# Forgetting attention: one 128-row matmul for the two score products that hold a low part

## The reference, cut to what matters

```python
fq = rms_norm(split_heads(fq, FOX_HEADS), fox_q_norm)
fk = rms_norm(split_heads(fk, FOX_HEADS), fox_k_norm)
...
s = jnp.einsum("bhqd,bhkd->bhqk", qb, kb) * scale
s = s + log_forget_cum[:, :, qs:qe, None] - log_forget_cum[:, :, None, :qe]
p = jax.nn.softmax(jnp.where(mask, s, -jnp.inf), axis=-1)
outs.append(jnp.einsum("bhqk,bhkd->bhqd", p.astype(v.dtype), v[:, :, :qe]))
```

## Time and profile before

| | us |
|---|---|
| median of 3 runs | 2940.7 |
| lowest and highest | 2927.48, 2946.58 |
| span of the profiled execution | 2942.3 |
| PE busy in it | 2806.3 (95%) |
| DVE, ACT, POOL busy | 1078.9, 664.0, 747.4 |

### The profile page before, as it was taken

The page is one execution under the profiler, slowest core; times in us unless marked ns, Lnnn a source line. Parts: engine busy times, 40 slices in busy tenths (PEclk is TensorE's granted clock), DMA queues, the critical chain, the costliest instruction groups (busy, mean ns, idle before and its releaser), DMA issues. The chain is left out here.

```text
span 2942.3 us, 37535 instructions
## 1 busy us (share of the span) xinstructions
PE 2806.3 (95%) x13970; PEld 2404.2 (82%) x13970; DVE 1078.9 (37%) x1994; ACT 664.0 (23%) x1237; POOL 747.4 (25%) x711
## 2 busy tenths in 40 slices
PE   7999999999979999998899998999879999999999
PEld 7999999999977878876577776888668888888887
DVE  5332222222554424242466663111142333333334
ACT  4111111110243223222344443112131111111110
POOL 3212211121132222221244445221232222222220
PEclk8999999999986858667799999999989999999999
DMA  3111111111110000000000001110312111111111
GB/s 125 58 44 48 54 44 44 44 44 37 55 61 1 23 22 0 1 1 28 8 6 3 5 1 65 43 50 14 116 44 64 43 58 43 43 57 43 43 36 58
DMA packets 32463, 115.67 MB, mean 39 GB/s; under 512 B 4000, under 2 KB 5920, under 8 KB 32208
## 3 DMA queue, kind: packets, MB, share of 16 engines
q1 hardware_dynamic: 32336, 113.90, 11.6%
HBM read 105.09 MB, written 8.65 MB: 39 GB/s over the span
## 5 line engine op out<-in xcount | busy, mean ns | idle before, releaser
L52 PE MATMUL f_bank<-u_hi,f_w_hi 128*128 128x346 f32 (+2 forms) x1760 | 618.5, 351 | 15.9 <-POOL u_lo L211 13.2
L53 PE MATMUL f_bank<-u_hi,f_w_lo 128*128 128x346 f32 (+2 forms) x1760 | 619.4, 352 | 0.0
L54 PE MATMUL f_bank<-u_lo,f_w_hi 128*128 128x346 f32 (+2 forms) x1760 | 618.8, 352 | 0.0
L424 POOL TENSOR_TENSOR f_w_lo<-f_raw,f_w_hi 128x1024 fp32r<-128x1024 f32 x132 | 326.9, 2496 | 1126.2 <-ACT f_w_hi L366 1126.0
L52 PEld LDWEIGHTS f_bank<-u_hi,f_w_hi 128*128 128x128 f32 x1760 | 332.5, 189 | 48.9 <-issue 17.0
L53 PEld LDWEIGHTS f_bank<-u_hi,f_w_lo 128*128 128x128 f32 x1760 | 332.3, 189 | 30.8
L54 PEld LDWEIGHTS f_bank<-u_lo,f_w_hi 128*128 128x128 f32 x1760 | 332.8, 189 | 30.0
L502 DVE TENSOR_TENSOR f_work<-f_work,f_bank 128x346 f32<-128x346 f32 (+2 forms) x110 | 64.4, 585 | 798.2 <-PE f_bank L54 788.1
L52 PE MATMUL f_bank<-f_hid_hi,f_w_hi 128*128 128x346 f32 (+2 forms) x880 | 309.0, 351 | 0.0
L53 PE MATMUL f_bank<-f_hid_hi,f_w_lo 128*128 128x346 f32 (+2 forms) x880 | 308.9, 351 | 0.0
L54 PE MATMUL f_bank<-f_hid_lo,f_w_hi 128*128 128x346 f32 (+2 forms) x880 | 308.9, 351 | 0.0
(11 more groups left out here) (279 smaller groups left out, 4571.6 us busy)
## 6 DMA issues: line engine op xcount, KB each, us to landing
f_raw<-in_ffn SPq DMA_DIRECT2D x132, 512.0 KB, 3.4
gt_raw<-in_gate SPq DMA_DIRECT2D x24, 512.0 KB, 3.5
fox_raw<-in_fox SPq DMA_DIRECT2D x12, 512.0 KB, 4.4
kept_hsave<-h_in SPq DMA_DIRECT2D x1, 4160.0 KB, 13.0
h_out<-kept_hsave SPq DMA_DIRECT2D x8, 520.0 KB, 6.6
ld_xin<-in_x SPq DMA_DIRECT2D x8, 512.0 KB, 4.4
op_raw<-in_wout SPq DMA_DIRECT2D x8, 512.0 KB, 5.7
out<-f_raw SPq DMA_DIRECT2D x6, 512.0 KB, 3.7
```

The source lines that it names most:

```text
L52: nc.tensor.matmul(out, w_hi, x_hi, start=first, stop=False)
L53: nc.tensor.matmul(out, w_lo, x_hi, start=False, stop=False)
L54: return nc.tensor.matmul(out, w_hi, x_lo, start=False, stop=last)
L424: nc.gpsimd.tensor_tensor(w_lo[:, slot, :], raw[:, raw_slot, :], w_hi[:, slot, :].bitcast(F32), ALU.subtract).then_inc(wlo_done, 1)
```

## The change

The low parts get tiles of 128 rows. `q_both` holds the high part of q in rows 0 to 63 and its low part in rows 64 to 127; `k_both` holds the low part of k in rows 0 to 63 and its high part in rows 64 to 127. One matmul over all 128 rows then adds up both products. ACT makes a second copy of each high part into these tiles.

```diff
         q_hi = [sb(f"q_hi{i}", [KALL, T], F32R) for i in range(2)]
-        q_lo = [sb(f"q_lo{i}", [DK, T], F32R) for i in range(2)]
+        q_both = [sb(f"q_both{i}", [P, T], F32R) for i in range(2)]
         k_hi = [sb(f"k_hi{i}", [KALL, T], F32R) for i in range(2)]
-        k_lo = [sb(f"k_lo{i}", [DK, T], F32R) for i in range(2)]
+        k_both = [sb(f"k_both{i}", [P, T], F32R) for i in range(2)]
@@ split_hi, on ACT
                     for j in range(2):
-                        last = nc.scalar.copy((q_hi if is_q else k_hi)[j][0:FOX_D, t0:t0 + n],
-                                              x32[:, 2 * (u % 2) + j, 0:n])
+                        x = x32[:, 2 * (u % 2) + j, 0:n]
+                        nc.scalar.copy((q_hi if is_q else k_hi)[j][0:FOX_D, t0:t0 + n], x)
+                        again = q_both[j][0:FOX_D] if is_q else k_both[j][FOX_D:P]
+                        last = nc.scalar.copy(again[:, t0:t0 + n], x)
                     last.then_inc(xhi_done, 1)
@@ scores_open, on PE
                     wait(pe, exp_done, p, PW, w - 2 if w >= 3 else 0)
-                    kh, kl = k_hi[h][0:DK, k0:k0 + P], k_lo[h][0:DK, k0:k0 + P]
-                    nc.tensor.matmul(out[:, 0:n], kl, q_hi[h][0:DK, q0:q0 + n], start=True, stop=False)
-                    nc.tensor.matmul(out[:, 0:n], kh, q_lo[h][0:DK, q0:q0 + n], start=False, stop=False)
+                    nc.tensor.matmul(out[:, 0:n], k_both[h][:, k0:k0 + P], q_both[h][:, q0:q0 + n],
+                                     start=True, stop=False)
@@ split_lo, on DVE
-                    hi, lo = (q_hi, q_lo) if is_q else (k_hi, k_lo)
+                    hi = q_hi if is_q else k_hi
                     wait(dve, xhi_done, p, NU, u + 1)
                     for j in range(2):
-                        last = nc.vector.tensor_tensor(lo[j][0:FOX_D, t0:t0 + n], x32[:, 2 * (u % 2) + j, 0:n],
+                        lo = q_both[j][FOX_D:P] if is_q else k_both[j][0:FOX_D]
+                        last = nc.vector.tensor_tensor(lo[:, t0:t0 + n], x32[:, 2 * (u % 2) + j, 0:n],
                                                        hi[j][0:FOX_D, t0:t0 + n].bitcast(F32), ALU.subtract)
                     last.then_inc(qk_done, 1)
```

## The result

| | before | after |
|---|---|---|
| median, us | 2936.74 (4 runs) | 2798.75 (4 runs, 2793.63 to 2804.32) |
| ratio | | 0.9526, 95% interval 0.950 to 0.9552 |
| span of the profiled execution | 2942.3 | 2797.2 |
| its mean granted clock | 0.918 | 0.964 |

The change saves 138 us of 2937; the profiled spans differ by 145.

A forecast was written before the change was run, and what follows sets the result against it. The prediction took forgetting attention's scores to be bound by TensorE at half clock. Scores 123 plus projection starts 8 minus ACT's copies 3 gave 128 us saved, 2942.3 - 128 = 2814.3, so 2814 us (range 2785 to 2835).

The forecast's parts named there:

- The gaps: Forgetting attention's scores: 0.58 us beyond streaming in each unit where PE changes between 64 rows and more, removed by the change.
- The rival that had another cause for them: Scores: the 0.58 us hang on something else and stay, only the removed product is saved, 2913 us; chance 0.05.
- The removed product: Scores: one of two products a unit goes, 0.427 us at 512 columns, 31.6 us over 8 heads at half clock.
- the case that the forecast took as the likeliest: Scores: full clock returns from about unit 8 on in each pair, giving 2814 us; recovery has chance 0.66.
- The term: One pair's scores after the change take 40.5 us in place of 71.3, saving 30.8 a pair, 123 in all.
- the 1.27 us a unit: Scores at full clock: price of the exponential, rounding and low-part chain, from 2.53 us; latent attention's is 1.65.
- ACT's copies: Projections: late copies cost 1.5 us a pair, 0.8 comes back at the opens, net 3 us over four pairs.
- The 8 us: Next pair's projections begin at full clock instead of 5.1 us at half: 2.6 x 3 = 8 us saved.
- Half clock throughout: Scores: something that remains holds the clock at 0.5, 85 us saved, 2857 us; chance 0.16.
- the half-way case: Scores: the clock comes back only in the long units, some 2840 us; chance 0.10.
- The slower case: Projections: ACT's copies take the clock from them, up to 110 us slower, 3050, or 2960; chance 0.03.
- The thin end below the forecast: Scores: clock never falls at the start, chain keeps its first price, 34 us a pair, 2788; below 2780 chance 0.05.

The follow-up runs named there:

- experiment 1: The kernel before with its two score products over 66 rows in place of 64, the added rows zero: 2810.89 us, ratio 0.9562.
- experiment 4: The kernel before without the product of k's high part by q's low part, the other low-part product left at 64 rows: 2901.74 us, ratio 0.9884.
- experiment 3: The changed kernel with one further product of 64 rows and 16 columns after each 128-row product: 2914.76 us, ratio 0.992.
- experiment 2: The changed kernel with its 128-row product made twice, six products a unit as before: 2797.41 us, ratio 0.9522.
- the second profile: The changed kernel run and profiled once more, nothing altered: 2806.53 us, ratio 0.9527.
- experiment 5: The changed kernel without ACT's second copies, their halves of the tiles holding ones: 2795.45 us, ratio 0.9502.
- experiment 7: The changed kernel with the second copies of the high parts made by DMA in place of ACT: 2801.66 us, ratio 0.9511.
- the other pair of versions: The changed kernel with DMA copies and every second low part of the weights on DVE, 2788.49 us; the same with all 112 128-row products made twice, 2792.76 us.

## Why the prediction was right, point by point

**What bounds it.** TensorE at half clock in the scores: shown. With the gaps gone (experiment 1) the 285 us fall to 166, with only a product gone (experiment 4) they fall only to 254, at half clock.

**The gaps.** 0.58 us a unit, tied to the change between 64 rows and more: shown by experiments 1, 3 and 4. The forecast had this cause only from places in the order, and it named them loosely: two of the four long steps are not at a change of height but one product behind it (L1158 to L1159, both 64 rows, and L1170 to L1185, 68 to 128). The rival that had another cause for them, such as the bank, is out, since experiment 1 changes rows alone. The Trainium skill, in "TensorEngine Tiling (Array Packing)", Key Properties, says that a change of the tiling mode drains TensorE; it does not say that an ordinary product over 64 rows counts as such a mode. If it does, the trace agrees: 0.13 us on the way in, 0.12 on the way out, and behind each change 0.16 to 0.17 that fits a load that was not hidden. The rule on weight loads of the Trainium skill, "TensorE: Matmul & The Clock Gate", Part 3, that I weighed in the forecast does not hold at full clock either: 128-row products of 512 columns stand 0.23 us apart.

**The removed product.** The forecast's sum for a clock that stays at half held 31.6 us for it, and experiment 4 gave 31.5. But telling the gain as product plus gaps holds at half clock only. In the case that the forecast took as the likeliest, the clock back, the product is worth nothing that these runs can tell (experiment 2), and the gaps and the clock are what counts.

**The clock.** It comes back, as forecast. The reason, that gaps and not thin products hold it down, was only half said in the forecast, and in the expectation of experiment 3 I even bet the other way. Experiment 3 shows it: 16 columns of 64 rows a unit suffice to keep it at half for most of the time. Height may have a smaller part: with 66 rows the scores take 166.1 us, 58 of them at half clock, with 128 rows and as many products 151.3, 17 of them at half clock (experiments 1 and 2). That rests on one profile of each, while two profiles of the changed kernel gave 150.4 and 156.0 with 27 and 48 us at half clock, so it is open.

**Where the time at full clock goes.** The term was 40.5 us a pair, measured 37.6 on average, 11.6 us too much over four; in the second profile 39.0, 6.0 too much. Most of it lies in units 0 to 7, for which the forecast had 12 us. They took 11.8, 9.7 (1002.51 - 992.79), 11.2 and 8.1 us, 10.2 on average: the clock was at half for 17.1 us of the scores in the first pair, 3.4 in the second, 6.8 in the third and not at all in the fourth. The rest of a pair, forecast at 28.5, took 27.4 (11.4 and 27.6 in the second profile). That it came so near is in part luck, since the chain of ACT, DVE and POOL does not run at the 1.27 us a unit that the sum leant towards. These are the exponentials, DVE's roundings and POOL's low parts of three 512 units in the second pair:

```profile
1001.75 1.28 POOL L971 TENSOR_TENSOR fox_p_lo<-fox_p,fox_p_hi 128x512 fp32r<-128x512 f32 x1 [0.93 <-DVE fox_p_hi L1329]
1002.18 1.12 DVE L1329 CAST fox_p_hi<-fox_p 128x512 fp32r<-128x512 f32 x1 [0.30 <-ACT fox_p L1049]
1003.05 0.60 ACT L1049 ACTIVATE fox_p<-fox_bank 128x512 f32<-128x512 f32 x1 [0.90 <-POOL fox_p_lo L971]
...
1003.38 1.29 POOL L971 TENSOR_TENSOR fox_p_lo<-fox_p,fox_p_hi 128x512 fp32r<-128x512 f32 x1 [0.36 <-DVE fox_p_hi L1329]
...
1003.68 1.26 DVE L1329 CAST fox_p_hi<-fox_p 128x512 fp32r<-128x512 f32 x1 [0.29 <-ACT fox_p L1049]
...
1004.70 0.60 ACT L1049 ACTIVATE fox_p<-fox_bank 128x512 f32<-128x512 f32 x1 [1.05 <-POOL fox_p_lo L971]
```

POOL's operations start 1.63 us apart, the exponentials 1.65: latent attention's price, not 1.27. The rounding takes 0.42 us when POOL is idle; here it takes 1.12 and 1.26 and ends 0.27 us after POOL's operation ends. It is not so in every unit. Of 42 such roundings of 512 columns that the timeline lists one by one, 19 began while POOL's subtraction was running, and all 19 ended 0.27 to 0.34 us after it; the other 23 took 0.42 to 0.43. In the kernel before, none of the 48 began while POOL was running. I had read the 2.53 us from a case in which POOL was idle while DVE rounded the 512 columns, and had halved it as if two units overlapped freely. The next unit's rounding, of 400 columns, stood in the same trace of before and had the other price:

```profile
899.83 1.18 DVE L1327 CAST fox_p_hi<-fox_p 128x400 fp32r<-128x400 f32 x1
```

It began under POOL's subtraction of 899.52 to 900.78 and ended 0.23 us after it. The page "SBUF — State Buffer" of the Trainium skill, section "SBUF: two separate sides", says that DVE, in the modes that use two ports, and GpSimd share a pair of ports, and that the one which starts first holds it for its whole instruction. The trace agrees in that a rounding that begins second ends only after POOL's operation; that it then needs 0.27 us more and not its whole 0.42 the page does not explain. The pair's price still came out near, since the forecast took a value between the two ends.

**ACT's copies.** Forecast 1.5 us a pair with 0.8 back, measured 2.0 a pair (experiment 5), 8.2 in all, of which PE's longer wait ahead of the maxima is 1.6 a pair. Place and sign were right: experiment 7 removes it by leaving the copies to DMA. The 8 us that the forecast counted for the starts of the last three pairs at full clock show in the projections of experiment 5: 154.4 us in these pairs against 164.2 before, 9.8.

**The sum.** 123 + 8 - 3 = 128 forecast; 134.8 + 2.4 = 137 measured in forgetting attention. The scores gave 12 us more than their 123, the projections 2.4 in place of 8 - 3 = 5. The likeliest case was the one that came; the term that was off most is the pair's price with the clock back, by 2.9 us. The 138 us between the medians lie close to the 137 by chance in part: between the profiled spans it is 145, and 9 of these lie behind forgetting attention, where the change does nothing.

**The rivals.** Half clock throughout did not come, though experiment 3 shows a kernel that is near it, nor did the half-way case: the clock is at half for 27 of 150 us. The slower case did not come either: the projections' clock stayed at 0.96 to 1.00. The thin end below the forecast, 34 us a pair with a clock that never falls, was not the pairs' mean: only the fourth came near it, with 34.7 us at 1.00.

## What to carry to other kernels

Look at the distance between starts, not at TensorE's busy share: a stretch called fully busy had 0.58 of each 3.16 us in gaps, and with these changes of height in each unit its clock stayed at half. Where products of 64 rows stand between higher ones, make them higher, with two rows of zeros if nothing better is at hand, before counting products; here that alone gave a ratio of 0.956, where the whole change gives 0.953. And price an overlap from a case where the other engine runs as well, not from one where it is idle.

## What of the hardware was unexpected

- One product of 16 columns with 64 rows in a unit of five others cost 116 us over 112 units, with a clock of 0.52 to 0.63 in the scores in place of 0.79 to 1.00. How much is the clock and how much the gaps themselves was not measured apart.
- 112 additional products of up to 512 columns cost nothing that could be told (2797.41 against 2798.75; in the other pair of versions 2792.76 against 2788.49, intervals overlapping).
- DVE's rounding of 128x512 took 0.42 us alone; begun under POOL's subtraction, it ended 0.27 to 0.34 us after that one, in 19 of 19 cases, and so took up to 1.49.
- The same stages ran 12.5 us longer in one profile of one kernel than in another, at a mean clock of 0.89 against 0.92 in the stretch where it shows. Why the clock falls in one execution and not in the other stays open.
